# Hybrid decoder layer on one core: NSA's compressed steps in slots of their own, another beginning, a narrow projection in two parts, and GpSimd writing low weight parts

## The reference, cut to what matters

```
a = RMSNorm(h)
(nq, nkv, ngate, dq, dk, dv, fq, fk, fv, ff, mg) = split(a @ w_in)
o_a = NSA(nq, nkv, ngate)        # compressed + selected blocks + sliding window
o_b = differential attention(dq, dk, dv)
o_c = forgetting attention(fq, fk, fv, ff)
merged = sum over three mixers of sigmoid(mg_i) * (o_i @ w_br_i)
h = h + merged @ w_o
h = h + conv_ffn(RMSNorm(h))     # up -> causal conv of width 3 -> gelu * gate -> down
```

```
s_c = q . k_cmp - slope * dist_c ;  p_c = masked_softmax(s_c) ;  o_c = p_c . v_cmp
o = gc0 * o_c + gc1 * o_s + gc2 * o_w
```

## Time and profile before

| | before |
|---|---|
| median of three runs | 978.65 us |
| the three runs | 976.17, 978.8, 978.65 us |
| the profiled execution, its time | 978.79 us |
| the profiled execution, its span | 977.0 us |
| TensorE busy | 958.5 us (98% of the span) |
| VectorE, ScalarE, GpSimd busy | 559.8, 426.2, 209.8 us |

### The profile page before, as it was taken

The page is one execution under the profiler, slowest core; times in us unless marked ns, Lnnn a source line. Parts: engine busy times, 40 slices in busy tenths (PEclk is TensorE's granted clock), DMA queues, the critical chain, the costliest instruction groups (busy, mean ns, idle before and its releaser), DMA issues.

```text
span 977.0 us, 12185 instructions
## 1 busy us (share of the span) xinstructions
PE 958.5 (98%) x4625; PEld 794.5 (81%) x4625; DVE 559.8 (57%) x1063; ACT 426.2 (44%) x770; POOL 209.8 (21%) x250
## 2 busy tenths in 40 slices
PE   6999999999999999999999999999999999999998
PEld 5787877788888888888888888888888888888887
DVE  6737787864366895546567454655655665522113
ACT  5335776754256653445777333423222322221110
POOL 3000457640001112212455220121112121100000
PEclk9999999999999999999999999999999999999999
DMA  6512110112222212222211242223222322232222
GB/s 237 219 44 86 45 44 1 43 45 86 87 89 85 87 44 87 86 87 87 81 50 44 87 172 87 87 89 123 91 87 87 121 95 86 87 117 99 87 87 86
DMA packets 13691, 86.33 MB, mean 88 GB/s; under 512 B 1473, under 2 KB 1985, under 8 KB 4289
## 3 DMA queue, kind: packets, MB, share of 16 engines
q1 hardware_dynamic: 13632, 85.55, 24.2%
HBM read 83.44 MB, written 2.10 MB: 88 GB/s over the span
## 4 chain that ended last, share of the span: by engine, by line
PE 89%; DVE 7%; ACT 2%; issue 2%; DMA 0%; SPq 0%; ACTq 0%; DVEq 0%
PE ps L1531 22%; PE ps L1533 22%; PE ps L1532 22%; PE ps L1715 10%; PE ps L1559 4%; PE ps L1672 1%; PE ps L1671 1%; PE ps L1700 1%; DVE prob_n L1232 1%; DVE wl L1013 1%; PE ps L1586 1%; DVE ptn_l L1267 1%; PE ps L1793 1%; PE ps L1795 1%; DVE prob L1232 1%
## 5 line engine op out<-in xcount | busy, mean ns | idle before, releaser
L1013 DVE TENSOR_TENSOR wl<-raw,wh 128x512 fp32r<-128x512 f32 (+2 forms) x118 | 173.5, 1475 | 136.4 <-ACT wh L701 133.8
L701 ACT ACTIVATE wh<-raw 128x2048 fp32r<-128x2048 f32 (+1 forms) x58 | 109.4, 1886 | 157.9 <-PE ps L1533 140.3
L1531 PE MATMUL ps<-aT_h,wh 128*128 128x512 f32 (+1 forms) x376 | 146.7, 390 | 0.8 <-DVE aT_l L1022 0.8
L1532 PE MATMUL ps<-aT_l,wh 128*128 128x512 f32 (+1 forms) x376 | 146.4, 389 | 0.0
L1533 PE MATMUL ps<-aT_h,wl 128*128 128x512 f32 (+1 forms) x376 | 146.4, 389 | 0.0
L1531 PE MATMUL ps<-wh,aT_h 128*128 128x512 f32 x256 | 102.0, 398 | 0.0
L1533 PE MATMUL ps<-wh,aT_l 128*128 128x512 f32 x256 | 100.0, 391 | 0.0
L1532 PE MATMUL ps<-wl,aT_h 128*128 128x512 f32 x256 | 99.8, 390 | 0.0
L1514 POOL TENSOR_TENSOR gl<-gl,rstdT 128x512 f32<-128x512 f32 x22 | 44.5, 2022 | 234.5 <-ACT gl L987 234.5
L1470 POOL TENSOR_SCALAR prob_n<-prob_n,coef 128x384 f32<-128x384 f32 (+3 forms) x64 | 67.7, 1071 | 114.6 <-DVE coef L1249 114.3
L1531 PEld LDWEIGHTS ps<-aT_h,wh 128*128 128x128 f32 (+1 forms) x376 | 70.0, 186 | 16.5 <-issue 1.0
(11 more groups left out here) (250 smaller groups left out, 1796.1 us busy)
## 6 DMA issues: line engine op xcount, KB each, us to landing
raw<-wblk SPq DMA_DIRECT2D x72, 1024.0 KB, 4.7
x<-x SPq DMA_DIRECT2D x4, 512.0 KB, 5.2
w_sb<-w SPq DMA_DIRECT2D x1, 2048.0 KB, 9.2
hid<-x SPq DMA_DIRECT2D x1, 2048.0 KB, 7.7
out<-outt SPq DMA_DIRECT2D x8, 256.0 KB, 2.0
stage<-consts SPq DMA_DIRECT2D x1, 708.5 KB, 4.7
later<-consts SPq DMA_DIRECT2D x1, 448.0 KB, 5.4
par<-params SPq DMA_DIRECT2D x1, 204.5 KB, 8.3
```

The costliest lines, as they stand in the source:

```text
L701: nc.scalar.activation(wh[b % 2][:, 0:n], raw[b % RING][:, 0:n], ACT.Copy).then_inc(hi_ready, 4)
L1013: ins = nc.vector.tensor_tensor(wl[b % RING][:, cols], raw[b % RING][:, cols], wh[b % 2][:, cols].bitcast(f32), ALU.subtract)
L1531: nc.tensor.matmul(dst, a_h, b_h, start=start, stop=False)
L1532: nc.tensor.matmul(dst, a_h, b_l, start=False, stop=False)
```

## The change

It has four parts.

**The beginning.** SyncE loads `par` ahead of block 0, and block 0 in four pieces with a semaphore each. VectorE scales only the first half of the tiles 0 to 2 (and both of tile 3); GpSimd scales the second half of the tiles 0 and 1, ScalarE that of tile 2. TensorE begins with 36 transposes of the identity, whose result nobody reads. In `cmp` the passes of a k stand in another order: both halves of h·h as soon as `aT_h` is there, then those with the low weights, and those with `aT_l` last.

**The narrow projection.** For `small`, the high and low weights of a k lie side by side as 64 columns (`small_w`), so that one matmul with `aT_h` gives h·h in PSUM rows 0 to 31 and l·h in rows 32 to 63, and a second one with `aT_l` adds h·l: 16 matmuls where there were 24. The two halves are added by the four following small matmuls with `id2`, two identities on top of each other, that stand in place of the transposes.

**The compressed steps.** SC keeps its slot; VectorE's part is an event of its own (SCV) one slot later, ScalarE's exponential (SCA) two later, CN three later; TC stands one slot later than before, and its copies (TCH, TCL) one slot behind it. `t_lag` of NSA goes from 5 to 6.

**Low weight parts.** VectorE no longer writes the low parts of the blocks 8 to 11 (`POOL_LO`); GpSimd does, 4 pieces each, between its scalings, in the places that the event list gives. TensorE waits for them on a semaphore of their own (`low`).

```diff
+POOL_LO = [BI[(NSA, "gate1")] + n for n in range(1, 5)]
...
-    t_lag, o_lag = {NSA: (5, 10), DIFF: (3, 5), FOX: (3, 5)}[m]
+    t_lag, o_lag = {NSA: (6, 11), DIFF: (3, 5), FOX: (3, 5)}[m]
...
-            put(per * i + 5, "CN", i)
-            put(per * i + 7, "TC", i)
+            put(per * i + 4, "SCV", i)
+            put(per * i + 5, "SCA", i)
+            put(per * i + 6, "CN", i)
+            put(per * i + 8, "TC", i)
+            put(per * i + 9, "TCH", i)
+            put(per * i + 9, "TCL", i)
...
+        def low(eng, b):
+            if b in POOL_LO:
+                eng.wait_ge(lo_pool, POOL_LO.index(b) + 1)
+            else:
+                eng.wait_ge(lo_ready, b + 1 - sum(p < b for p in POOL_LO))
         def bank(key):
             return ps[place[key][0]]
+        def small_w(b):
+            return wh[b % 2][:, 0:KD * 64].rearrange("p (k r c) -> p k r c", r=2, c=32)
...
-            load(0)
             sp.dma_start(par[:, :], params).then_inc(par_in, 16)
+            for piece in range(4):
+                cols = slice(piece * 512, piece * 512 + 512)
+                sp.dma_start(raw[0][:, cols], wblk[0, :, cols]).then_inc(first_in[piece], 16)
...
+            act.wait_ge(rstd_ready, TT - 1)
+            nc.scalar.activation(xn0[:, 2, S:D], x0[:, 2, S:D], ACT.Copy, scale=rstd[:, 2:3]).then_inc(xa_ready, 1)
...
-                for half in range(2):
+                for half in range(2 if t == TT - 1 else 1):
...
-                    elif what == "WL":
+                    elif what == "WL" and j not in POOL_LO:
                         split(j, e[2])
-                    elif what == "SC":
+                    elif what == "SCV":
...
+            for t in range(2):
+                pool.wait_ge(rstd_ready, t + 1)
+                nc.gpsimd.tensor_scalar(xn0[:, t, S:D], x0[:, t, S:D], rstd[:, t:t + 1], None, ALU.mult).then_inc(xp_ready, 1)
+            pool.wait_ge(id_in, 16)
+            nc.gpsimd.tensor_copy(id2[0:32, :], ident[0:32, 0:32]).then_inc(id2_ready, 1)
+            pool.wait_ge(id2_ready, 1)
+            nc.gpsimd.tensor_copy(id2[32:64, :], ident[32:64, 32:64]).then_inc(id2_ready, 1)
             pool.wait_ge(par_in, 16)
+            pool.wait_ge(id2_ready, 2)
...
-            for j, u in enumerate(units_of(NSA)):
-                p = scores_at(NSA, j, span(u)[1])
-                pool.wait_ge(coef_ready, j // 2 + 1)
-                nc.gpsimd.tensor_scalar(p, p, coef[:, j:j + 1], None, ALU.mult).then_inc(pn_scaled, 1)
+            for e in EVENTS[NSA]:
+                if e[0] == "C":
+                    for j in (e[1] - 1, e[1]):
+                        p = scores_at(NSA, j, span(units_of(NSA)[j])[1])
+                        pool.wait_ge(coef_ready, j // 2 + 1)
+                        nc.gpsimd.tensor_scalar(p, p, coef[:, j:j + 1], None, ALU.mult).then_inc(pn_scaled, 1)
+                elif e[0] == "WL" and e[1] in POOL_LO:
+                    b, piece = e[1:]
+                    cols = slice(piece * 512, piece * 512 + 512)
+                    pool.wait_ge(hi_ready, 4 * b + piece + 1)
+                    ins = nc.gpsimd.tensor_tensor(wl[b % RING][:, cols], raw[b % RING][:, cols], wh[b % 2][:, cols].bitcast(f32), ALU.subtract)
+                    if piece == 3:
+                        ins.then_inc(lo_pool, 1)
             full(pool, ("TA", len(STEPS) - 1))
+            pool.wait_ge(lo_pool, len(POOL_LO))
...
+                    pe.wait_ge(id2_ready, 2)
                     bk = begin(("ST",))
                     for t in range(TT):
-                        ins = nc.tensor.transpose(bk[:, 32 * t:32 * t + 32], smT[:, t * P:(t + 1) * P], ident[0:32, 0:32])
+                        ins = nc.tensor.matmul(bk[:, 32 * t:32 * t + 32], smT[:, t * P:(t + 1) * P], id2[:, :], start=True, stop=True)
...
+            for n in range(36):
+                nc.tensor.transpose(ps[5][:, 0:P], ident[:, :], ident[:, :])
             for t in range(TT):
                 for k in range(KD):
-                    if k % 4 == 0:
-                        pe.wait_ge(xn_ready, 2 * t + k // 4 + 1)
+                    if k == 0:
+                        pe.wait_ge(xn_ready, t + 1)
+                    elif k == 4:
+                        pe.wait_ge(*((xp_ready, t + 1) if t < 2 else (xa_ready, 1) if t == 2 else (xn_ready, TT + 1)))
...
-                        if k % 2 == 0:
-                            pe.wait_ge(*((first_lo, k // 2 + 1) if k < 6 else (lo_ready, 1)))
-                        free(pe, ("N", 0, k))
-                        for c in range(2):
-                            key = ("P", m, "cmp", c)
-                            bk = begin(key) if k == 0 else bank(key)
-                            cols = slice(c * P, (c + 1) * P)
-                            ins = passes(bk[:, :], h[:, k, cols], l[:, k, cols], aT_h[:, k], aT_l[:, k], k == 0, k == KD - 1)
-                            if k == KD - 1:
-                                done(key, ins)
-                    h, l = weights(BI[(m, "small")], KD, 32)
+                        pe.wait_ge(hi_ready, k // 2 + 1)
+                        pe.wait_ge(hi_taken, hi_at[("N", 0, k)])
+                        for part in range(3):
+                            if part == 1 and k % 2 == 0:
+                                pe.wait_ge(*((first_lo, k // 2 + 1) if k < 6 else (lo_ready, 1)))
+                            if part == 2:
+                                free(pe, ("N", 0, k))
+                            for c in range(2):
+                                key = ("P", m, "cmp", c)
+                                bk = begin(key) if k == 0 and part == 0 else bank(key)
+                                cols = slice(c * P, (c + 1) * P)
+                                ins = nc.tensor.matmul(bk[:, :], (l if part == 1 else h)[:, k, cols], (aT_l if part == 2 else aT_h)[:, k],
+                                                       start=k == 0 and part == 0, stop=k == KD - 1 and part == 2)
+                                if k == KD - 1 and part == 2:
+                                    done(key, ins)
+                    pe.wait_ge(lo_ready, BI[(m, "small")] + 1)
+                    w = small_w(BI[(m, "small")])
                     bk = begin(("P", m, "small", 0))
                     for k in range(KD):
-                        ins = passes(bk[0:32, :], h[:, k], l[:, k], aT_h[:, k], aT_l[:, k], k == 0, k == KD - 1)
+                        if k:
+                            nc.tensor.matmul(bk[0:32, :], w[:, k, 0], aT_l[:, k], start=False, stop=False)
+                        ins = nc.tensor.matmul(bk[0:64, :], w[:, k].rearrange("p r c -> p (r c)"), aT_h[:, k], start=k == 0, stop=k == KD - 1)
+                        if k == 0:
+                            nc.tensor.matmul(bk[0:32, :], w[:, k, 0], aT_l[:, k], start=False, stop=False)
```

51 lines of the change are left out of this document (32 added, 19 removed).

## The result

The changed kernel took 980.1 us (median of 22 runs, 978.0 to 987.55) against 978.24 us of the kernel before (22 runs, 975.51 to 979.0) on the same chips: ratio 1.003, 95% interval 1.0022 to 1.0039. It is slower by 1.9 us where 972.0 was forecast, and lies outside the range of 967 to 978. The profiled execution took 981.16 us with a span of 979.4.

What follows compares the result with a forecast made beforehand. TensorE, busy 958.5 of 977.0 us, was taken as the bound. Terms -1.3 - 0.95 - 2.0 - 1.3 + 0.3 - 1.7 = -6.95 from 978.79 us gave 971.8, stated as 972.0; range 967.0 to 978.0.

Steps and rivals of the forecast that it cites:

- What bounds the kernel: Whole kernel: TensorE bounds it, busy 958.5 of 977.0 us; after 208 us the change moves no work.
- The compressed steps: NSA's units: TensorE's two waits for CN's result, 2.0 us, go because other work lies in between; -2.0 us, bound 0.
- late next: NSA's units: SC needs the bank osum_n frees (0.6 us in two waits); their distance shrinks from two slots to one.
- one of the conditions for being wrong: NSA's units: the forecast is wrong if SC waits longer for osum_n than the sum of waits removed.
- the 0.08 on the slower side: Whole kernel: chance of a slower result, 0.07 for GpSimd becoming the bound and 0.01 for anything unseen.
- The start: Beginning up to the first product: bank 0 full 0.4 us earlier, 0.9 us wait for aT_l gone; -1.3 us, bounds -2.0 and 0.
- The narrow projection: The small projection: 16 matmuls for 24 save 1.85 us, a wait takes 0.9, id2 costs nothing; -0.95 us, bound -1.85.
- Low parts on GpSimd: NSA's units: lighter VectorE cuts TensorE's waits by 1.3 us, bounds -2.5 and 0; GpSimd's load costs +0.3, bounds 0 and +5.8.
- The clock: NSA's units: one of two half-speed dips, both behind a pause before SC, goes; -1.7 us, bounds -3.4 and +1.7.
- The rivals: Waits only change hands (0.20, 976.5); GpSimd becomes bound (0.07, 986); everything goes (0.12, 968); transposes don't raise clock (0.03, 976.0).
- the waits only change hands: Rival, NSA's units: waits on VectorE remain, only start and narrow projection gain 2.3 us; 976.5 us, chance 0.20.

Runs made afterwards that it cites:

- e1: The kernel before with only the compressed steps in slots of their own and t_lag, o_lag at 6 and 11: 980.34 us, ratio 1.0025.
- e5: The changed kernel with t_lag, o_lag back at 5 and 10, the compressed steps left in their own slots: 979.78 us, 1.0041 to the kernel before.
- e9: The changed kernel with SC and TC of tiles 1 to 3 in the spare gate bank, at slots chosen per tile: 973.42 us, 0.9954 to the kernel before.
- e3: The kernel before with only the other beginning: 977.18 us, ratio 0.9997.
- e12: The kernel before with x scaled on VectorE, narrow projection by 64-row transposes and VectorE's add, compressed steps of e9, low parts left on VectorE: 972.29 us, 0.9942.
- e2: The kernel before with only the low parts of blocks 8 to 11 on GpSimd: 976.9 us, ratio 0.9992.
- e14: e12 with a wait for VectorE's newest ptn_l in front of SC of tiles 2 and 3: 975.7 us, 0.9993 to the kernel before.
- e15: e12 with the wait for the newest ptn_l in front of gate matmuls of 512 columns, slots 31 and 49: 974.17 us, 0.9969 to the kernel before.
- e13: e12 with the low parts of blocks 8 to 11 on GpSimd: 971.89 us, 0.9949 to the kernel before.

## Why the prediction was wrong, point by point

**What bounds the kernel.** Right: only NSA's units and what stands ahead of them moved; the rest is 760.6 us in every trace.

**The compressed steps (-2.0, measured about +3.6).** This is the step that failed. The text said that "what was waited for has a slot of other work in between" and took all of it. The distance from CN to TC was two slots before and is two slots after. What the new slots shortened is ScalarE's wait for `pc` ahead of CN (at tile 1 from 2.16 to 0.92 us), and TensorE didn't wait for that. TensorE runs some two slots ahead of VectorE, so two slots are no distance at all: it had reached TC of tile 1, slot 24, at 125.92 us, when VectorE had CN, slot 22, still to do. The waits for `pc` went from 2.0 to 3.3. And what the prediction itself had flagged as "late next" came: SC came nearer to `osum_n`, and its wait went from 0.6 to 2.9, 2.3 us more. "From two slots to one" was right for tile 2 alone: by the event list it is from three to two for tile 1, where there is no wait, and from one to none for tile 3. I had written that the lighter VectorE offsets it. It doesn't, since the wait consists of a chain (`ptn_h`, `otmp_n`, `ptn_l`, `osum_n`) and no low part stood in it (2.9 in e1 too). e1 shows both waits with nothing else changed; e5 removes the one by the distance alone; e9 removes both with another bank and more distance. The two waits alone grew by 3.6; all waits of the units grew by 3.4. That one of the conditions for being wrong was precisely this sum should have given it more than the 0.08 on the slower side.

**The start (-1.3, measured +0.2 in this pair, +0.5 on average).** Two faults. "The product no longer waits for VectorE's `aT_l`" was false: `cmp` writes to banks 6 and 7, which hold x transposed for k 0 and 1 and are freed by exactly these two `aT_l`. The reordering made it worse, since the second matmul now needs the second bank 0.56 us after the first, where three passes stood before. That was to be read from the plan of the banks. Second, GpSimd's scalings were taken as 1.55 us and took 1.85 and 2.38 (e3: 2.37 and 1.58). Undisturbed the price was right: the same size takes 1.57 in NSA's units. It is GpSimd that gave way: VectorE's square at 8.37 us began 0.02 us behind its landing, in the middle of GpSimd's scaling, and took its usual 0.69, while the scaling stretched. The clock came up early as forecast, but in e3 it fell again.

**The narrow projection (-0.95, measured -1.0 and +0.64).** The wait on `wl` (0.7 us, 0.9 forecast) and the 4.55 us are nearly as worked out. "`id2` costs four small matmuls for four small transposes, nothing" was the wrong sentence: in f32 each goes through twice, eight of 0.126 us against four of 0.09.

**Low parts on GpSimd (-1.3 and +0.3 for GpSimd, measured +0.9 alone at the same clock, at most -0.4 on top of e12).** The pieces took 1.26 to 1.30 us (one 1.39) as priced, and with `t_lag` at 6 TensorE waited for no scaling; with 5 it waits 0.9 (e2, e5). But the "8.3 of its 83.75 busy us" that were to leave VectorE did so in part only: `coef` grew from 5.2 to 10.2 us in the changed kernel. And what was taken off lies in slots where TensorE didn't wait for it: the wait moved to TC of tile 3. The sum of VectorE's busy time was no measure of the gain.

**The clock (-1.7, measured 0).** 6.8 us at half speed before and after, in one stretch instead of two. A dip costs half its length, as forecast: less waits and half of the half-speed time, the units take 101.0 us in e2 with no dip and 101.1 in the kernel before with two. One pair of profiles hides how often it happens: of the 113 executions of the kernel before made beside the experiments 40 are at 1.0, of the changed kernel's 22 none (its slowest, 987.55 us, has a mean of 0.988). The kernel before takes 975.4 to 976.7 us at 1.0 and 978.5 to 979.2 at 0.996. So part of the 1.9 us by which the medians differ is a rarer full clock, which the forecast had the other way. That it follows SC is not so (e14, e15); that long waits and dips go together is seen at the other end: with the units' waits at 4.6 to 4.8 us and none above 0.9, none of three profiles (e9, e12, e13) has one, all 16 of their executions are at 1.0, and their times scatter by 0.5 us instead of 3.

**The rivals.** None of them is what happened. The nearest, "the waits only change hands", held for its reason and still left the start and `id2` as gains, and its price had no growth of the sum in it. A case "SC waits for `osum_n`" (978.8 + 2.3 + 1.3, less 0.4 of the narrow projection and nothing for the start) would have given 982.

## What to carry to other kernels

Count distances in a hand-written order from the instruction that frees the bank or makes the operand to the one that needs it, and subtract how far the waiting engine runs ahead; a step that is at most one slot behind its releaser waits, on whichever engine (here `osum_n`, `pcT` and the gate's ScalarE step in turn). Before taking a wait as gone, look up who else must release the same bank. And taking load off an engine pays only where it is waited for: twelve subtractions fewer on VectorE were worth 0.4 us at most and came with a loss of 0.9 where the slots were left as they were; 4 us of waits removed by other slots and another bank were worth 7 with the clock that came with them.
